# A hybrid decoder block: branch products of one column block between the gate products of the next, and regions moved in memory

## The reference

```
q, k, v, xr, yr, ga, gl = split_cols(rmsnorm(x) @ w_in)
y_attn = sliding_window_attention(q, k, v, sinks) @ w_attn_o
y_lru = (rg_lru(conv(xr)) * gelu(yr)) @ w_lru_o
merged = sigmoid(ga) * y_attn + sigmoid(gl) * y_lru
x = x + merged @ w_out
```

## Time and profile before

| | us |
|---|---|
| median of 3 runs | 2152.6 (2151.63 to 2152.64) |
| profiled execution | 2151.84 |
| its span | 2150.2 |
| TensorE busy | 2004.9 (93%) |
| VectorE busy | 1598.8 (74%) |
| ScalarE busy | 1293.9 (60%) |
| mean granted clock of TensorE | 0.973 of full |

### The profile page before, as it was taken

How to read it: one execution, slowest core, us unless ns; L and a number is a source line. 1 busy time by engine, 2 the same in 40 slices (tenths; PEclk the granted TensorE clock), 3 DMA queues, 4 the chain that set the end, 5 groups by cost and what they waited for, 6 DMA issues and landing times.

```text
span 2150.2 us, 37083 instructions
## 1 busy us (share of the span) xinstructions
PE 2004.9 (93%) x11768; PEld 1532.1 (71%) x11769; DVE 1598.8 (74%) x2100; ACT 1293.9 (60%) x1755; POOL 290.8 (14%) x334
## 2 busy tenths in 40 slices
PE   6999899999898399999999999999999999999993
PEld 5777677777687277777777777777777777777772
DVE  4778755545655488797877779977878988977894
ACT  5555454444533267676665667766667767755774
POOL 3100000000124201111112111121101101210100
PEclk9999999999998699999999999999999999999996
DMA  5020111010634769798888889978889979878994
GB/s 175 20 98 1 40 40 40 20 39 1 215 133 140 170 219 378 279 341 313 286 291 291 283 290 380 375 264 286 287 290 377 376 260 375 311 258 285 377 339 165
DMA packets 256003, 489.57 MB, mean 228 GB/s; under 512 B 20043, under 2 KB 38311, under 8 KB 255856
## 3 DMA queue, kind: packets, MB, share of 16 engines
q1 hardware_dynamic: 233824, 439.56, 57.2%
q0 software_dynamic: 21088, 49.35, 8.7%
q10 hardware_dynamic: 1040, 0.00, 0.0%
HBM read 461.01 MB, written 32.05 MB: 229 GB/s over the span
## 4 chain that ended last, share of the span: by engine, by line
PE 80%; DVE 7%; issue 4%; ACT 4%; DMA 2%; SPq 1%; POOL 0%; ACTq 0%; DVEq 0%; POOLq 0%
PE psum L749 15%; PE psum L750 14%; PE psum L753 14%; PE psum L766 8%; PE psum L455 3%; PE psum L585 3%; PE psum L589 3%; PE psum L587 3%; PE psum L457 2%; PE psum L456 2%; PE psum L737 2%; PE psum L692 1%; PE psum L716 1%; DVE o_lo L1490 1%; PE psum L693 1%
## 5 line engine op out<-in xcount | busy, mean ns | idle before, releaser
L1679 DVE TENSOR_TENSOR w_lo<-ring,w_hi 128x1024 fp32r<-128x1024 f32 x768 | 914.9, 1221 | 142.8 <-ACT w_hi L1056 131.5
L1056 ACT ACTIVATE w_hi<-ring 128x1024 fp32r<-128x1024 f32 x768 | 803.6, 1059 | 275.1 <-PE psum L753 265.9
L749 PE MATMUL psum<-w_hi,rows_hi 128*128 128x512 f32 x1024 | 422.1, 412 | 4.2 <-DVE rows_lo L1683 2.5
L750 PE MATMUL psum<-w_hi,rows_lo 128*128 128x512 f32 x1024 | 399.9, 391 | 0.0
L753 PE MATMUL psum<-w_lo,rows_hi 128*128 128x512 f32 x1024 | 316.2, 390 | 0.0
L749 PEld LDWEIGHTS psum<-w_hi,rows_hi 128*128 128x128 f32 x1024 | 193.8, 189 | 46.7 <-issue 10.3
L753 PEld LDWEIGHTS psum<-w_lo,rows_hi 128*128 128x128 f32 x1024 | 192.5, 188 | 41.1
L750 PEld LDWEIGHTS psum<-w_hi,rows_lo 128*128 128x128 f32 x1024 | 193.2, 189 | 37.5
L749 PE MATMUL psum<-w_hi,act_hi 128*128 128x512 f32 x512 | 219.8, 429 | 0.0
L750 PE MATMUL psum<-w_hi,act_lo 128*128 128x512 f32 x512 | 202.8, 396 | 0.0
L766 PE MATMUL psum<-ring,region_m 128*32 128x256 f32 x3072 | 174.2, 380 | 0.0
(11 more groups left out here) (333 smaller groups left out, 2997.7 us busy)
## 6 DMA issues: line engine op xcount, KB each, us to landing
ring<-in_w_gate_up_dram SPq DMA_DIRECT2D x128, 2048.0 KB, 16.1
ring<-in_w_down_dram SPq DMA_DIRECT2D x64, 2048.0 KB, 14.1
ring<-in_w_in_dram SPq DMA_DIRECT2D x16, 512.0 KB, 5.2
region_m<-in_x_dram SPq DMA_DIRECT2D x8, 512.0 KB, 11.6
ring<-in_w_in_dram SPq DMA_DIRECT2D x2, 2048.0 KB, 17.5
ring<-in_w_out_dram SPq DMA_DIRECT2D x2, 2048.0 KB, 7.5
region_a<-in_x_dram POOLq DMA_DIRECT2D x8, 512.0 KB, 4.8
acc_rows<-region_a POOLq DMA_DIRECT2D x8, 512.0 KB, 3.3
```

The lines of the kernel that those rows point to most:

```text
L749: mm(bank(i), hi[:, ks], wh, start=(k0 + q == 0), stop=False)
L750: mm(bank(i), lo[:, ks], wh, start=False, stop=False)
L1056: act.activation(w_hi[:, n % NBUF, :], place[i][:, k0 * HALF:(k0 + 2) * HALF], ACT.Copy).then_inc(hi_done, 1)
L1679: v.tensor_tensor(out=w_lo[:, n % NBUF, :], in0=place[i][:, k0 * HALF:(k0 + 2) * HALF], in1=w_hi[:, n % NBUF, :].bitcast(f32), op=ALU.subt ...
```

## The change

It touches three things.

- **Order on TensorE.** Blocks 0 to 6: four branch pieces of block j (`LEAD`), then the gate pieces of block j + 1 with two branch pieces of j behind each of the first six (`PER_GATE`). Block 7: all branch pieces at the end, as before. ScalarE's and VectorE's lists are rewritten to the same order, and the merge of j now stands on VectorE behind the last remainders of that weave and the first one of block j + 1, ahead of its second and third.
- **Order of the four sigmoids**: by branch and then by half, and the merge waits for all four.
- **Order of the regions**: region_s and region_a come right behind ring, region_m last. All three, and ring, then start on a multiple of 128 bytes. Before, region_s and region_a started 64 bytes past one. What lies behind the regions (ident, mask and the small tables) keeps its addresses.

```
-        at_m = next_base()
-        region_m = sb("region_m", [P, LM * (SEQ + 3) + LM * SEQ])
         at_s = next_base()
         region_s = sb("region_s", [P, LM * SEQ])
         at_a = next_base()
         region_a = sb("region_a", [P, A_COLS])
+        at_m = next_base()
+        region_m = sb("region_m", [P, LM * (SEQ + 3) + LM * SEQ])
...
+LEAD = 4
+PER_GATE = (2, 2, 2, 2, 2, 2, 0, 0)
...
             for j in range(KD):
-                if j >= 1:
-                    pe.wait_ge(sgate_done, 4 * j)
-                if j >= 1:
-                    for k in range(KD):
-                        gate_piece(j * KD + k)
...
+                if j == KD - 1:
+                    out_pieces(j, 0, 16)
+                    break
+                out_pieces(j, 0, LEAD)
+                done = LEAD
+                for k in range(KD):
+                    if k == 0:
+                        pe.wait_ge(sgate_done, 4 * (j + 1))
+                    gate_piece((j + 1) * KD + k)
+                    out_pieces(j, done, done + PER_GATE[k])
+                    done += PER_GATE[k]
...
+            for j in range(KD):
+                last = j == KD - 1
+                if not last:
+                    gate_high((j + 1) * KD)
+                sigmoids(j)
+                out_high(16 * j + 3)
+                if last:
+                    for p_ in range(4, 16):
+                        out_high(16 * j + p_)
+                    break
+                gate_high((j + 1) * KD + 1)
+                out_high(16 * j + 4)
+                out_high(16 * j + 5)
+                weight_high(8 * (j + 1))
+                weight_high(8 * (j + 1) + 1)
+                for k in range(2, KD):
+                    gate_high((j + 1) * KD + k)
+                    if k < KD - 1:
+                        out_high(16 * j + 2 * k + 2)
+                        out_high(16 * j + 2 * k + 3)
+                    weight_high(8 * (j + 1) + k)
+                for p_ in range(OBUF):
+                    out_high(16 * (j + 1) + p_)
...
+                for k in range(2, KD):
+                    gate_low((j + 1) * KD + k)
+                    if k < KD - 1:
+                        out_low(16 * j + 2 * k + 2)
+                        out_low(16 * j + 2 * k + 3)
+                    weight_low(8 * (j + 1) + k)
+                out_low(16 * (j + 1))
+                merge(j, 0)
+                merge(j, 1)
+                out_low(16 * (j + 1) + 1)
+                out_low(16 * (j + 1) + 2)
```

More of the change, by code:

```diff
@@ L627, in _, with out_pieces @@
             pe.wait_ge(lru_done, LM)
-            for j in range(KD):
-                if j >= 1:
-                    pe.wait_ge(sgate_done, 4 * j)
-                if j >= 1:
-                    for k in range(KD):
-                        gate_piece(j * KD + k)
[L636 to L649, removed]
+            def out_pieces(j, lo_, hi_):
+                for p_ in range(16 * j + lo_, 16 * j + hi_):
+                    r, th = p_ // 2, p_ % 2
+                    k, q = r // 2 % GROUP, r % 2
+                    if p_ == 0:
+                        pe.wait_ge(pT_done, 2 * NT)
+                    if p_ == 16 * j and j >= 1:
+                        pe.wait_ge(merged_done, 2 * j)
+                    pe.wait_ge(o_lo_done, p_ + 1)
+                    lo = (wao_lo, wlo_lo)[q][:, k, j * P:(j + 1) * P]
+                    three(out_bank(th, q), ow_hi[r % 8], lo, o_hi[p_ % OBUF], o_lo[p_ % OBUF],
+                          k == 0, k == GROUP - 1).then_inc(o_mm, 1)
+            for j in range(KD):
+                if j == KD - 1:
[9 more added lines that the diff above has]
+                    done += PER_GATE[k]
             pe.wait_ge(merged_done, 2 * KD)
@@ L972, in out_high, with sigmoids @@
                 act.activation(o_hi[p_ % OBUF], (oT, lruT)[q][:, k, th * HALF:(th + 1) * HALF], ACT.Copy).then_inc(o_hi_done, 1)
[L974 to L982, removed]
+            def sigmoids(j):
                 act.wait_ge(gate_mm, KD * (j + 1))
@@ L985, in _ @@
                     act.wait_ge(merged_done, 2 * j)
-                for th in range(2):
-                    for q in range(2):
+                for q in range(2):
+                    for th in range(2):
                         act.activation(sgate[th][q], bank(2 + 2 * th + q), ACT.Sigmoid).then_inc(sgate_done, 1)
[L989 to L993, removed]
+            gate_high(6)
+            weight_high(0)
+            gate_high(7)
+            for r in range(1, 8):
+                weight_high(r)
+            for p_ in range(OBUF):
+                out_high(p_)
+            for j in range(KD):
[19 more added lines that the diff above has]
+                    weight_high(8 * (j + 1) + k)
+                for p_ in range(OBUF):
+                    out_high(16 * (j + 1) + p_)
             def h2T_out(t):
@@ L1534, in _, with merge @@
                 gate_low(n)
-            for j in range(KD):
[L1536 to L1547, removed]
+            def merge(j, th):
+                dve.wait_ge(o_mm, 16 * j + 12 + th + 1)
+                dve.wait_ge(sgate_done, 4 * j + 4)
+                mg = merged[:, j, th * HALF:(th + 1) * HALF]
+                v.tensor_tensor(out=mg, in0=sgate[th][0], in1=bank((6 + 2 * th) % 8), op=ALU.mult)
+                dve.wait_ge(o_mm, 16 * j + 14 + th + 1)
+                then(v.tensor_tensor(out=sgate[th][1], in0=sgate[th][1], in1=bank((7 + 2 * th) % 8), op=ALU.mult))
+                v.tensor_tensor(out=mg, in0=mg, in1=sgate[th][1], op=ALU.add).then_inc(merged_done, 1)
@@ new lines, in _ @@
+            gate_low(6)
+            weight_low(0)
+            gate_low(7)
+            for r in range(1, 8):
+                weight_low(r)
+            for p_ in range(OBUF):
+                out_low(p_)
+            for j in range(KD):
+                last = j == KD - 1
+                if not last:
+                    gate_low((j + 1) * KD)
+                out_low(16 * j + 3)
+                if last:
+                    for p_ in range(4, 16):
+                        out_low(16 * j + p_)
```

14 lines of the change are left out of this document (6 added, 8 removed).

## The result

The changed kernel takes 2133.6 us (median of 4 runs, 2130.4 to 2136.8) against 2152.6 before (2151.6 to 2153.7): a ratio of 0.9911, 95% interval 0.9894 to 0.9929, 19 us less. The profiled execution is the lowest of the four, 2130.38 us with a span of 2128.8. The forecast was 2128.

What follows compares the result with a forecast made beforehand. TensorE, busy 93% of the span, was taken as the bound. Weave 11.8 plus addresses 12.9 (experts 8.9, output projection 2.5, branch products 1.5) gave 24.7 us off, forecast 2128 us, range 2121 to 2141.5.

Steps and rivals of the forecast that it cites:

- The weave's size: Gate/branch blocks 0 to 6: weaving removes the holes after the fourth branch piece, 11.8 us over seven blocks.
- loses 3.3 - 1.6 = 1.7: Per gate/branch block: 3.3 us of waiting shrinks to a 1.5 us hole plus 0.1 for slower restart.
- The branch products' pace: Branch products: 384 matmuls each 4.7 ns faster from new addresses, less pieces that wait anyway, 1.5 us.
- The output projection: Output projection, m_hi loaded from region_s: 384 matmuls each 6.6 ns faster from new addresses, 2.5 us.
- The experts: Expert products on act: faster from new addresses, 10.2 us less 1.3 lost to waits for VectorE, 8.9 us.
- 1536 x 6.7 ns: Expert products on act: every one of 1536 matmuls gains 6.7 ns, 10.2 us.
- The cause given for the addresses: region_s and region_a started 64 bytes past a multiple of 128; starting on one gives TensorE 0.227 us, 12.9 us in all.
- the transposes: Counter-evidence on addresses: 128-column transposes from region_m and region_a both last 272 ns; weighed less for their shorter stream.
- Rival 1: Addresses do nothing; act products are slower for what goes on beside them: 2140.8 us, chance 0.11.
- rival 5: Weave and addresses both nil, the merge late by 1.7 us: 2152.6 us, chance 0.03.
- Rivals 2 and 4: 2: restarts between kinds, 2136.4, or later merge, 2139.7, chance 0.07; 4: merge up to 5.4 us later, 2166, chance 0.03.
- Rival 3: More than forecast: 18.4 us for the addresses, or the fourth branch piece comes sooner: 2122 us, chance 0.06.

Runs made afterwards that it cites:

- e1: The changed kernel with the regions back in their old order and the woven order kept: 2142.7 us, ratio 0.9952.
- e2: The kernel before with the new order of the three regions and nothing else: 2146.3 us, ratio 0.9963.
- e5: The changed kernel with act_hi and act_lo moved by 128 bytes and ow_hi by 64: 2137.2 us (single run).
- e8: The changed kernel with a 64-byte pad ahead of ring, so ring and all regions move by 64 bytes: 2130.3 us, ratio 0.9904.
- e4: The changed kernel with act_hi, act_lo, o_hi and o_lo moved by 64 bytes and ow_hi by 128: 2139.5 us (single run).
- e6: The changed kernel with act_hi and act_lo moved by 32 bytes and ow_hi by 64: 2134.6 us (single run).
- e9: The changed kernel with act_hi and act_lo moved by 256 bytes and o_hi, o_lo and ow_hi by 128: 2133.2 us (single run).
- e10: The changed kernel with act_hi and act_lo moved by 512 bytes and ow_hi alone by 128: 2132.1 us (single run).
- e3: The changed kernel with LEAD = 3 and PER_GATE = (3, 2, 2, 2, 2, 2, 0, 0): 2125.4 us, ratio 0.9874.

## Why the prediction was right or wrong

**What bounds the kernel, and the weave's mechanism: right.** The holes behind the fourth branch piece went and the one ahead of it stayed (3.62 us for 3.6). The merge ended at the moment of the last gate product, TensorE's first piece waited the forecast 0.2 us for it, and the block did not. A change between gate and branch products costs nothing: from the last branch product of a pair to the next gate product it is 0.228 us, like any other step.

**The weave's size: 10.2 us for 11.8.** The step "loses 3.3 - 1.6 = 1.7" measured 1.46 in e1, where the operands are still in their old places. By the step a block of e1 would be 96 x 0.227 + 48 x 0.231 + 1.6 = 34.5 us and was 34.7; with the operands in their new places, 144 x 0.227 + 1.6 = 34.3, it was 34.36. So the holes were sized rightly. The 0.2 us that e1 has too much lies between the gate products (20.42 us for 20.20): the prediction took it that an operand off its place slows its own product alone, and woven in, the branch products slow the gate products behind them too. Among themselves they go at 0.231 in e1, as I had read.

**The branch products' pace: 2.4 us for 1.5.** 34.70 to 34.36 seven times. What the first term missed, this one has, and for the same reason. Together the two terms of the blocks are 12.6 for 13.3.

**The output projection: 2.4 us for 2.5.** The number fits in part by luck: 0.4 of the 2.4 is a shorter time at the lower clock, and the pace gave 2.0 (103.9 to 101.9 with the slow steps taken off), or 2.1 in e2, where as many steps are slow as before.

**The experts: 4.3 us for 8.9.** This is the term that was mis-sized, and nearly all of the forecast's miss of 5.6 us. The step that failed is "1536 x 6.7 ns". By pieces 16 to 23 of a step without tail, the median gained 28, -27, 20, -19, 12, 40, 23 and 39 ns. Only pieces 21 and 23 have the 40 ns (6 x 6.7) that I took for all. The pieces that begin behind transposes or a bias product gained less; e2's rows show that behind a restart the new place doesn't give 0.227 either. Piece 17 hands its gain to the wait for VectorE, as the prediction subtracted; piece 19 hands one back too, which it did not: the transposes behind it start later after its start than before (1.51 us for 1.49 in the step at 1024.6), so something there ends at a time of its own; what, is open. The sum is 0.11 us a step without tail and 0.20 with, instead of 0.24 and 0.32, in all 4.8; the first 16 pieces of a step without tail took 0.03 us longer than before, which takes 0.5 of it back. I had measured one steady piece and multiplied it by all.

**The cause given for the addresses: wrong, and lucky.** The rows showed that region_a's operands are slow and region_m's are not; that the multiple of 128 is what tells them apart was an inference from the change's own words, and e5 and e8 refute it. What counts is where the operands start relative to each other modulo 256 bytes. The forecast held although its cause was wrong, because the new order happens to put all four regions at 128 modulo 256 as well as on multiples of 128. The argument against it, the transposes, was worth little: they follow each other after 109 ns in all twelve traces.

**Against the Trainium skill.** "SBUF — State Buffer", section "Door 1: The DMA port swizzle", has lines of 16 bytes as the unit for a reader, under which 32, 64 and 128 bytes more are all alike. For the absolute place the runs agree (e8, nothing changed); for the place of one operand relative to the other they don't (e4 to e6, e9, e10). "TensorE: Matmul & The Clock Gate", section "Step-by-step: what each phase is for", has the loading of the next operand cost the running product nothing. Here moving the loaded operand alone (ow_hi in e10) costs 0.3 us a block, by what path the runs don't show.

**Rivals.** Rival 1 (addresses do nothing) is excluded by e2, and rival 5 (nothing at all) by the result. Rivals 2 and 4 needed restarts or a late merge, and the timeline shows neither. Rival 3 was right in one thing: the fourth piece can come sooner, by 1.24 us a block, but it took e3 to do so.

## What to carry to other kernels

Where one engine's stretch is fed by two others in series and the stretch beside it leaves those idle, weave the two; then look for what is left behind the longest single step of a feeder, and put a piece that doesn't need it there (e3: 8 us for two numbers). In a stretch that waits a faster instruction gained nothing (e2), so an address gain shows only once the schedule has made the engine the bound: try such parts alone and together. Before multiplying a pace by a count, read it at the first piece behind each interruption as well as in mid-run. And before crediting a stage's gain to a change, look whether the clock at its start was the same.

## What the runs showed of the hardware

- Products of 128x128 by 128x512 in this three-product form, in mid-run at the full clock, follow each other after 0.227 us where all loaded and streamed operands start at the same place modulo 256 bytes of a partition. From branch product to branch product in the woven stage, waits left out, the mean step is 0.228 us after the change and in e8, 0.231 in e1 and e9, 0.232 in e4, 0.233 in e5 and e6, 0.235 in e10 (offsets of 64 and 128 bytes; 32 was tried with the act pieces, e6). The absolute start doesn't matter: with everything 64 bytes further the kernel took 2130.3 us.
- The slowness outlasts the product that is off: gate products with all operands in place take 0.2305 us on average for nine steps behind such branch products in e1 (0.232 in e9) and 0.227 from then on.
- Behind a wait with the clock at full, the first product lasts 0.50 us instead of 0.39 and the steps after it are some 0.235 in the good place too (e2, 375.29 to 376.23).
- Behind the 6.7 us in which TensorE idles ahead of the output projection, the granted clock is 0.50 (1.2 GHz) and products follow after 0.427 us, for six to twelve steps in the twelve traces.
- ScalarE's copies from either region took the same 632 ns, and transposes follow after 109 ns in every kernel.
